# A one-core diffusion layer on Trainium2: routing each tile inside the LayerNorm stage, and expert 0's rows summed by TensorE

## The reference

```
x1  = layer_norm(ALPHA * x + ga * mix, ln1_g, ln1_b)          # mix: (640 x 1024) @ w_out
h2  = x1 * (1 + cf) + sf                                      # input of the experts
g   = top-1 of softmax(h2 @ wg + bg)                          # 4 groups
e   = top-2 of softmax over the 4 experts of group g          # logits h2 @ we + be, 16 experts
gate= g_p * e_p / sum(e_p)
hid = h2 @ w_expert_in[e];  a, up = split(hid)                # 1024 x 512, per expert
y   = (silu(a) * up * gate) @ w_expert_out[e]                 # 256 x 1024, per expert
out = layer_norm(ALPHA * x1 + gf * sum_e y, ln2_g, ln2_b)
```

## Time and profile before

| | us |
|---|---|
| median of 3 runs | 669.38 (668.39 to 669.97) |
| the profiled execution | 673.35 |
| its span in the trace | 671.7 |

### The profile page before, as it was taken

The page is one execution under the profiler, slowest core; times in us unless marked ns, Lnnn a source line. Parts: engine busy times, 40 slices in busy tenths (PEclk is TensorE's granted clock), DMA queues, the critical chain, the costliest instruction groups (busy, mean ns, idle before and its releaser), DMA issues.

```text
span 671.7 us, 7754 instructions
## 1 busy us (share of the span) xinstructions
PE 524.8 (78%) x3102; PEld 436.5 (65%) x3102; DVE 363.8 (54%) x526; ACT 266.1 (40%) x366; POOL 138.4 (21%) x134
## 2 busy tenths in 40 slices
PE   3789999999899896888798974259999999993000
PEld 0567999987599885666687864247887777772000
DVE  1415131632020317778386554729998888961597
ACT  1515211112132216567411124018988778751231
POOL 0008200003000003120033333211222111001764
PEclk9987999999899999789898985559999999996555
DMA  8996983638343113772460007077999999981732
GB/s 299 389 329 173 301 319 126 247 129 264 127 146 122 56 72 94 315 201 52 127 248 33 33 31 281 8 275 276 399 404 401 402 405 398 405 320 67 247 105 114
DMA packets 67820, 146.74 MB, mean 218 GB/s; under 512 B 6510, under 2 KB 15273, under 8 KB 67528
## 3 DMA queue, kind: packets, MB, share of 16 engines
q1 hardware_dynamic: 54648, 108.93, 45.0%
q0 software_dynamic: 10400, 35.71, 15.2%
q10 hardware_dynamic: 2736, 1.61, 0.8%
HBM read 124.97 MB, written 21.25 MB: 218 GB/s over the span
## 4 chain that ended last, share of the span: by engine, by line
PE 45%; DMA 17%; DVE 17%; issue 10%; ACT 8%; SPq 1%; POOL 1%; ACTq 0%; DVEq 0%; POOLq 0%
DMA uni<-in_w_expert_out 10%; PE PS L1428 6%; PE PS L1429 6%; PE PS L1433 6%; PE PS L1373 6%; PE PS L1374 5%; PE PS L1375 5%; PE PS L1390 3%; DMA raw<-in_w_ada 2%; DMA g<-in_x_prompt 2%; DVE act_lo L1279 2%; DVE small L1098 2%; ACT act_hi L823 1%; DMA uni<-h_rows,uni 1%; DVE PS L1042 1%
## 5 line engine op out<-in xcount | busy, mean ns | idle before, releaser
L1373 PE MATMUL PS<-w_hi,act_hi 128*128 128x512 f32 x248 | 101.4, 409 | 3.9 <-DVE act_lo L1284 2.5
L1428 PE MATMUL PS<-act_hi,w_hi 128*128 128x320 f32 x320 | 100.3, 321 | 2.7 <-ACT g L675 1.7
L1429 PE MATMUL PS<-act_lo,w_hi 128*128 128x320 f32 x320 | 98.5, 315 | 0.0
L1374 PE MATMUL PS<-w_lo,act_hi 128*128 128x512 f32 x248 | 98.4, 397 | 0.0
L1375 PE MATMUL PS<-w_hi,act_lo 128*128 128x512 f32 x248 | 98.3, 396 | 0.0
L1148 DVE TENSOR_TENSOR w_lo<-raw,w_hi 128x2048 fp32r<-128x2048 f32 x32 | 73.0, 2285 | 4.2 <-ACT w_hi L816 4.0
L1433 PE MATMUL PS<-act_hi,w_lo 128*128 128x320 f32 x320 | 74.3, 314 | 0.0
L1428 PEld LDWEIGHTS PS<-act_hi,w_hi 128*128 128x128 f32 x320 | 62.0, 194 | 9.1 <-issue 4.5
L816 ACT ACTIVATE w_hi<-raw 128x2048 fp32r<-128x2048 f32 x32 | 61.1, 1912 | 14.6 <-DMA raw<-in_w_expert_in 14.5
L1429 PEld LDWEIGHTS PS<-act_lo,w_hi 128*128 128x128 f32 x320 | 62.1, 194 | 0.0
L1373 PEld LDWEIGHTS PS<-w_hi,act_hi 128*128 128x128 f32 x248 | 47.7, 192 | 16.3 <-issue 5.3
(11 more groups left out here) (223 smaller groups left out, 879.4 us busy)
## 6 DMA issues: line engine op xcount, KB each, us to landing
raw<-in_w_expert_in SPq DMA_DIRECT2D x32, 1024.0 KB, 14.4
raw<-in_w_ada SPq DMA_DIRECT2D x24, 1024.0 KB, 8.2
uni<-in_w_expert_out SPq DMA_DIRECT2D x16, 1024.0 KB, 15.0
raw<-in_w_in SPq DMA_DIRECT2D x12, 1024.0 KB, 8.6
expert_rows<-uni POOLq DMA_DIRECT2D x16, 512.0 KB, 7.1
expert_rows<-g POOLq DMA_DIRECT2D x2, 2560.0 KB, 11.6
g<-in_x_sample SPq DMA_DIRECT2D x2, 2048.0 KB, 14.8
raw<-in_w_out SPq DMA_DIRECT2D x4, 1024.0 KB, 9.2
```

Source lines behind the costliest of these rows:

```text
L1373: T.matmul(out, lh, rh, start=first, stop=False)
L1374: T.matmul(out, lh, rl, start=False, stop=False)
L1428: T.matmul(out, a, h_hi[:, k, sl], start=f, stop=False)
L1429: T.matmul(out, a, h_lo[:, k, sl], start=False, stop=False)
```

## The change

Five things are altered together.

1. **POOL does no arithmetic in the LN stage.** x1 is made by one DVE instruction (`times_gain`: minus mean, times gain) and one of ACT (times 1/std). The shift `ln1_b` is loaded again near the end (`x1_shift`) and added by DVE to all five tiles there. For the last two tiles `times_gain` and ACT's part lie behind expert 0's splits.
2. **The router runs tile by tile inside the LN stage.** `choose(n)`, `rank(n)`, `put(n)` and `fill(n)` do for one tile what was done for all five. Choosing uses DVE's max and max_index instructions, groups are padded to eight columns (24 logits instead of 20), and the counts so far are carried from tile to tile in `before`.
3. **Expert 0's rows are not gathered from DRAM.** `gather_first(n)` multiplies the 128 x 128 blocks of h2 of tile n with a one-hot matrix that DVE makes (`hot_0`), five tiles added up in PSUM. POOL gathers from expert 1 on. h2 of all tiles stays in SBUF for that (`h2_held`).
4. **The last tile goes in halves** through DVE, PE's transposes and ACT's copies.
5. **The tables that only overflow and the end need** are made in DVE's expert turns 1 to 5 (`LATER`), and PE's overflow list in turn 6.

The core of the diff, shortened:

```diff
             def expert_out(e):
                 slot = e % 2
-                if e == 0:
-
-                    sp.wait_ge(s_h2, NT)
-                    sp.wait_ge(s_x1, NT)
-                elif e >= 2:
+                if e < 2:
+
+                    sp.wait_ge(s_h2, H2)
+                    sp.wait_ge(s_h2t, NT)
+                    sp.wait_ge(s_h2s[2 * e], 16)
+                    if e == 1:
+                        sp.wait_ge(s_v, NT)
+                else:
                     sp.wait_ge(s_olo, e - 1)
...
             for n, t in enumerate(T_ORDER):
 
-                pool.wait_ge(s_xn, n + 1)
-                nc.gpsimd.tensor_tensor(x1[:, t, :], x1[:, t, :], ln1_g, ALU.mult).then_inc(s_plc, 1)
-                pool.wait_ge(s_h2, n + 1)
-                pool.dma_start(h2_dram[t * P:(t + 1) * P, :], h2_rows[:, n % 2, :]).then_inc(s_h2s[n % 2], 16)
-                pool.wait_ge(s_plc, n + 1)
-                nc.gpsimd.tensor_tensor(x1[:, t, :], x1[:, t, :], ln1_b, ALU.add).then_inc(s_x1, 1)
...
+            def choose(n):
+
+                lg = logits[:, n, :]
+                dve.wait_ge(s_lg, n + 1)
...
+                link(V.tensor_tensor(lg, PS[:, 0 if n == NT - 1 else 6, 0:NR], rb[:, :], ALU.add))
+                link(V.max(g_top[:, n, :], lg[:, 0:E_AT]))
+                link(V.max_index(g_at, g_top[:, n, :], lg[:, 0:E_AT]))
+                link(V.tensor_copy(g_num, g_at[:, 0:1]))
+                link(V.tensor_scalar(e_open, const[:, C_GROUP:C_GROUP + NE], g_num, -3.0e38, ALU.not_equal, ALU.mult))
+                link(V.tensor_tensor(e_open, e_open, lg[:, E_AT:NR], ALU.add))
+                link(V.max(e_top[:, n, :], e_open))
+                link(V.max_index(e_at, e_top[:, n, :], e_open))
...
+            def put(n):
+
+                dve.wait_ge(s_pos, n + 1)
...
+                V.tensor_tensor(slot_hot[:, n % 2], const[:, C_COL:C_COL + P].unsqueeze(1).to_broadcast([P, 2, P]),
+                                place[:, n, :].unsqueeze(2).to_broadcast([P, 2, P]), ALU.is_equal).then_inc(s_plr, 1)
+                dve.wait_ge(s_plr, n + 1)
+                link(V.tensor_scalar(hot_0[:, n, :], slot_hot[:, n % 2, 0, :], OH[:, n, 0, 0:1], None, ALU.mult))
...
+            def gather_first(n):
+
+                pe.wait_ge(s_o0, n + 1)
+                if n == 0:
+                    pe.wait_ge(s_mor, NT - 1)
+                    pe.wait_ge(s_zero, 1)
+                    for h in range(2):
+                        T.matmul(PS[:, 2 + h, :], zeros, ln1_g[:, 0:CH], start=True, stop=False)
                 for k in range(KD):
...
+                    mm = T.matmul(PS[:, 2 + k // 4, (k % 4) * P:(k % 4 + 1) * P], h2_held[n][:, k, :], hot_0[:, n, :],
+                                  start=False, stop=(n == NT - 1 and k % 4 == 3))
...
             mix_out(0)
             for n in range(1, NT):
                 mix_out(n)
-                router(n - 1)
+                turn_h2(n - 1)
+            gather_first(0)
+            gather_first(1)
+            router(NT - 2)
+            fill(NT - 3)
+            gather_first(2)
             turn_h2(NT - 1)
             router(NT - 1)
...
+            rank(NT - 2)
+            rank(NT - 1)
+            gather_first(NT - 2)
+            fill(NT - 2)
+            gather_first(NT - 1)
+            fill(NT - 1)
...
+            choose(NT - 2)
+            choose(NT - 1)
+            put(NT - 2)
+            put(NT - 1)
...
             expert_wlo(0, 0, 0)
+            gathered_lo(0, 0)
             expert_wlo(0, 0, 1)
-            gathered_lo(0, 0)
+            dve.wait_ge(s_ls, NT)
+            V.tensor_scalar(list_s[:, 0:NE], PS[:, 7, 0:NE], AWAY, None, ALU.add).then_inc(s_lc, 1)
...
+            times_gain(NT - 2)
+            times_gain(NT - 1)
...
+            LATER = {1: chunk_bases, 2: token_slots, 3: token_gates, 4: overflow_hots, 5: overflow_table}
```

More of the change, by code:

```diff
@@ L49, in build @@
     TW = DR * SPAN
+    NR = 24
+    E_AT = 8
+    AWAY = 4096.0
     PAIRS = HP * NB
@@ L440, in _ @@
                 expert_in(e, 1)
-            for e in range(2):
-                expert_out(e)
+            expert_out(0)
             for e in range(2, NE + 2):
@@ L1142, in expert_wlo @@
+                if n < NT - 2:
+                    times_gain(n)
+                if 1 <= n < NT - 2:
+                    put(n - 1)
             def expert_wlo(e, b, h):
@@ L1579, in mix_out @@
                     for k in range(KD):
-                        if n >= 1 and c == 1 and k == KD // 2:
-                            turn_h2(n - 1)
+                        if n >= 2 and (c, k) == (0, 4):
+                            router(n - 2)
+                        if n >= 3 and (c, k) == (1, 0):
+                            fill(n - 3)
+                        if n >= 2 and (c, k) == (1, 4):
+                            rank(n - 2)
                         mm = three(PS[:, 2 * (n % 2) + c, :], h_hi[:, k, ts], h_lo[:, k, ts], wh[:, k, :], wl[:, k, :],
@@ new lines, in rank, with fill @@
+            def rank(n):
+                pe.wait_ge(s_one, n + 1)
+                out = PS[:, 1 if n == NT - 1 else 6, 32:32 + NE]
+                T.matmul(out, tri, both[:, n % 2, :], start=True, stop=False)
+                T.matmul(out, ones[:, :], before[:, n % 2, :], start=False, stop=True).then_inc(s_pos, 1)
+            def fill(n):
+                pe.wait_ge(s_plr, n + 1)
+                for c in range(2):
+                    mm = T.matmul(PS[:, 7, 0:NE], slot_hot[:, n % 2, c, :], chunk_tok[:, n % 2, c, :],
+                                  start=(n == 0 and c == 0), stop=(n == NT - 1 and c == 1))
+                mm.then_inc(s_ls, 1)
```

487 lines of the change are left out of this document (281 added, 206 removed).

## The result

The changed kernel takes 654.84 us in the median of 4 runs (652.25 to 656.78), beside 669.34 us (668.39 to 669.97) for the kernel before: ratio 0.975 (95% interval 0.9713 to 0.9787), 14.5 us less. Timed twice more in the experiments it stood at 0.971 (0.9685 to 0.9734) and 0.9733 (0.9693 to 0.9772), 19.1 and 18.5 us less. One execution of the second timing, of 1588.75 us at a granted clock of 1.00, is out of the ratio; the median of 653.24 counts it and would be 653.08 without it. The profiled execution took 653.20 us, its span 651.4.

A forecast was written before the change was run, and what follows sets the result against it. Expert turns limited first by PE, later by the loads, behind a DMA hole. List -10.7, expert 1's split -19.3, -9.6 left at turn 4, -17.5 at the end: 669.38 - 17.5 = 651.9 us; range 645 to 661.

The forecast's parts named there:

- LN stage: PE's last product to end at 394.1 us instead of 396.4: 2.0, 1.7 and 0.8 off, 2.2 added.
- C: Rival, 6%: DVE limits the LN stage, max and max_index taking 0.71 us; 9 us lost, 661 us.
- The list: After the last product: list ready at 421.5 us instead of 432.2, -10.7 (bounds -9 to -12.4).
- The gather: After the list: expert 1's gather takes 9.00 us, its rows split at 434.8 instead of 454.1, -19.3.
- The tables: Expert turns 1 to 5: tables cost 9.7 us on DVE, leaving -9.6 us at turn 4.
- Two limits: Remaining turns: engines' limit gives -19.3 us, loads' limit -17.1; the loads decide, -17.5 taken.
- The median: Whole kernel: profiled execution of 673.35 us ran 4.0 above the median; 669.38 - 17.5 = 651.9.
- A: Rival, 20%: in the turns, loads keep the 10.29 us pace from turn 5 at once; -9.6 stays, 659.8 us.
- B: Rival, 14%: gather_first at full clock (-1.7), gather in 6 to 7 us (-2.5), 10.29 pace hardly appears; 646 to 643.
- D: Rival, 8%: DVE instructions with two SBUF inputs block POOL's descriptor writing at the first gather; 2.6 us more, 654.5.
- E: Rival, 4%: clock stays at half in the expert turns, PE's 9.21 us become 17 to 18; 680 us.
- F: Rival, 2%: the moves are hidden and nothing comes of them in the whole kernel; 669 us.

The follow-up runs named there:

- pool_arith: Changed kernel with two POOL multiplications by ones per tile put back for the LN stage's first three tiles; median 5.0 us above the changed kernel's.
- whole_tile: Changed kernel with the last LN tile computed, transposed and copied whole instead of in halves; ratio 0.9734 to the kernel before.
- tables_late: Changed kernel with the five tables moved to turns 9 to 13 and PE's overflow list to turn 14; ratio 0.9736 to the kernel before.
- best_three: Changed kernel with last tile's turn ahead of gather_first(2), list ahead of expert 0's row split, expert 2's second in-weights ahead of expert 1's out-weights; ratio 0.9684.
- first_by_pool: Changed kernel with expert 0's rows again gathered from DRAM by POOL instead of summed from one-hots; median +6.3 us.
- split_first: Changed kernel with second half of expert 0's weight split and the list ahead of expert 0's row split on DVE; ratio 0.9713 to the kernel before.
- best_early: Like best_three, but DVE splits expert 0's weights earlier, the first half between the last two choices, and times_gain for tile 3 precedes the list; ratio 0.971.

## Why the prediction was right, step by step

The forecast was 651.9 for the median; 654.84, 653.24 and 654.13 were measured. Against the kernel before the gain of 17.5 us was forecast, and 14.5, 19.1 and 18.5 were measured. The number came out although the wait for the gather was taken at twice its length; the limit by the loads, which it had foreseen, is what kept that from showing. That the other misses below come to less than 3 us in the median is luck.

- **LN stage.** The last product was to end at 394.1 and ended at 392.16. Of the 1.9 us difference 1.8 had arisen ahead of the stage (its first product began at 327.08, before at 328.88); from there it takes 65.1 us, where the sum gives 65.2. pool_arith shows the cause: VectorE's instructions stand behind POOL's, +4.0 us with three tiles' arithmetic, where the forecast's 2.0 of wait and 1.7 of clock are 3.7.
- **`choose`.** 14 small instructions at 0.23 were taken. The search for the largest values takes 0.17 or 0.18, that for their index 0.09 and 0.16; `choose(4)` ran from 405.55 to about 408.3, 2.8 instead of 3.2. C is out.
- **The last tile.** That turn(4) would wait for PE's queue was right (404.4 forecast, 402.35 measured), and whole_tile shows its consequence, which the prediction did not draw: the halves bring nothing that could be told.
- **The list.** 421.5 forecast, 420.4 measured, that is -11.8 instead of -10.7, and the middle value for the last two sums was right: one ran at half clock, one at full.
- **The gather.** This is the term that was most mis-sized: 9.00 us were taken over from the earlier trace rows, and 4.70 were measured. With the list's 1.1 that made expert 1's split 24.6 us earlier (429.5) instead of 19.3. The time falls into three parts. POOL's issue took 2.82 us before, beside two DVE splits, and 1.37 here. From its end to the first packet of the gather it was 3.4 us before and 0.7 here. From there to the landing it was 2.8 and 2.6. So the rows themselves move nearly as fast beside loads. In the middle part before, a load that SP issued 1.9 us behind the gather moved first. The queues of the kernel before, from 435.4 to 438.6 and from 438.7 to 441.5:

```profile
q1 hardware_dynamic: 448, 0.92, 92.0%
```

```profile
q0 software_dynamic: 166, 0.61, 58.4%
```

- **The tables.** 9.7 us were taken. From expert 1's split to the fifth L1279, behind all tables, the kernel before takes 43.5 us (452.87 to 496.34) and the changed one 51.6 (428.27 to 479.87): 8.1. tables_late gives 7.1 at the fifth, where it already waits for loads. So the fifth came 16.5 us earlier instead of 9.6, by the 5.3 of the split and the 1.6 of the tables. PE's overflow list, 2.29 us in turn 6, has no term in the prediction.
- **Two limits.** The step that saved the forecast: both the engines' and the loads' sums ended near 17 to 19, and the loads were said to decide. The loads' sum can be redone with the windows above: from 402 to 470 us 20.7 MB moved instead of 14.0, and 6.7 MB at 403 GB/s are 16.6 us, where the prediction had 15.8 less idle. What the gather and the tables gave more (16.5 instead of 9.6 at the fifth L1279) was not on top at the end: the last L1279 of the two profiled executions comes 20.3 us earlier, 1.8 of it from ahead of the LN stage, where 16.5 and the 9.7 that the engines were to give back would have been 26, or 24 with PE's list. In the turns at 10.2 us ACT waits for loads (7.6 us from 530 to 590). That the loads decide is read from these counts and waits; tables_late supports it for the middle turns only.
- **The median.** The prediction held the profiled execution of before (673.35) to be 4.0 above the median. In the three later sets the medians of before were 672.4, 673.9 and 672.6, so its execution was no outlier; the set that the median of 669.38 came from was the low one. Counted from the 672.6 of the last set, the same 17.5 would give 655.1. The 20.2 us between the two profiled executions are no better a measure of the change than the 14.5.
- **The end.** Unchanged, and the additions of ln1_b lie in DVE's wait, now 12.23 us (18.31 in the earlier trace rows).
- **Rivals.** A is out: six turns of 9.66 follow the fourth L1279. B came half true: the gather was quicker still than B had it, the sums' clock half of the time, and the loads' pace appeared all the same. D cost next to nothing: POOL's first issue took 1.37 us beside DVE's L1162 (1.09 in best_three, where it started ahead of that). Its second took 3.03 us beside the 2.3 us subtraction L1274 and 1.02 in first_by_pool with DVE idle, and nobody waited for it. Two SBUF inputs on DVE alone don't slow it so, for beside L1162 the second issue took 1.04 in best_three and 1.67 in split_first. E is out, the clock is 0.95 to 1.00 from 437.7. F is out.

By parts, as the medians of single experiments give them: POOL's arithmetic out of the stage 5.0 (4.0 of it seen in the stage), one-hots for expert 0 6.3, tables in the turns 3.2, halves 0.5 (from another set) with no certainty of its sign. They add up to about 15 of the 19.1 of the first set. Such parts need not add up, since the loads can hide some of them, and the router tile by tile was not tried alone, so what it is worth is not shown.

## What to carry to other kernels

When the loads set the pace of a long loop, ask of every microsecond saved ahead of it whether the loads start earlier too; in first_by_pool the loads were late with the rest, and the whole 7 us arrived at the end. Making an input ready sooner is worth nothing while the engine that is to use it has other work in its queue: look there before halving a tile. And the duration of a small gather is to be taken from a place with the same transfers beside it, not from the place where it was.

## What the runs showed that was not expected

- A gather of one expert's rows took 4.70 us with idle DMA engines at its start, 4.59 behind the tail of one load and with the next issued 1.7 us after it, 6.76 with one issued 0.9 us ahead of it, and 9.00 before the change. Most of the difference lies ahead of the first row: 0.6 to 0.7 us behind the issue's end in the two quick ones, 2.3 and 3.4 in the two slow ones. Its issue on POOL took 1.09 us in best_three and split_first, 1.37 in the changed kernel and 2.82 in the kernel before:

```profile
432.50 2.82 POOL L537 DMA_INDIRECT uni<-h_rows,uni  x1 [23.35 <-DVE uni L1274]
```
- Starting expert 0's product 2 us earlier can bring nothing at all: at clock 0.50 it takes 8.4 us instead of 5.6. The Trainium skill (TensorE: Matmul & The Clock Gate, Part 1) has the clock fall behind idle time. best_three and the changed kernel agree with that by 0.7 us more of idle time just ahead of the product, but best_early, with no more than the changed kernel, does not.
- PE enters the LN stage up to 3.4 us apart from run to run, in kernels that are alike up to there, and the stage then takes 64.1 us within 0.1 in all of the changed kernel's versions but pool_arith.
